# Query pairs taken earlier, keys ahead of the last rotated sum, and a head's ninth block turned later

## The chip, the cores and the metric

The kernel runs on one core of a Trainium2 chip. The metric is the time of one execution on the device in microseconds (us). Before the change it was 1448.48 us, the median of three runs (1446.67 to 1448.85).

Engine names in the rows: PE is TensorE (PEld its weight loads), DVE is VectorE, ACT is ScalarE, POOL is GpSimd, SP is SyncE, which issues most DMAs. Each works through its own queue of instructions in order, and they meet through semaphores.

## The reference

One step of a streaming encoder with two layers over 1024 prompt rows, 16 meta rows and 32 sample rows (1072 columns in all), 8 heads of width 128, in float32.

```
layer 0 (first attention, "fox"):
    h = rmsnorm(x);  q, k, v, f, g = h @ w_in;  logf = log_sigmoid(f + b)
    p = softmax(q k^T / sqrt(128) + cumsum(logf)_q - cumsum(logf)_k, causal)
    x = x + (p v * silu(g)) @ w_out
shared latent, once:
    ckr = rmsnorm(x) @ w_dkv;  c = rmsnorm(ckr[:256]);  kr = rope(ckr[256:320])
layer 1 (second attention, "mla"):
    p = rmsnorm(x) @ w_in
    q = rmsnorm(p[:384]) @ w_uq   ->  per head 128 plain + 64 rotated
    k, v = c @ w_ukv              (128 + 128 a head)
    p = softmax((q_plain k^T + rope(q_rot) kr^T) / sqrt(192), causal by chunks of 64)
    x = x + (p v * silu(gate)) @ w_out
y = rmsnorm(x);  outputs also k, v, logf of layer 0, c and kr
```

The sample rows attend to a cache of 512 rows as well.

## The kernel before

Every float32 operand of a large product is split into a high and a low part, and a product is three matmuls (`three_pass`, L75 to L82: high x high, high x low, low x high). ACT rounds the high part, DVE or POOL subtracts it to get the low part. The order of work on each engine is written out by hand, as loops over the same steps on all engines.

**Attention loops.** For each head h and query tile i (0 to 7, 128 queries; tile i sees i+2 blocks of 128 keys) the loop prepares the scores of the next tile (at i = 7 those of tile 0 of head h+1), turns the probabilities of tile i, and puts products of other kinds between (projections of the next head). In every second step PE also forms the values product of a pair of tiles; the last pair of a head, values(h, 3), comes in step (h+1, 0) behind scores(h+1, 1).

`turn_probs` transposes the probabilities in groups of four blocks (`prob_groups`, L69): 9 blocks at i = 7 make groups of 4, 4 and 1, at i = 4 to 6 there are two groups. Each group goes into one of two PSUM banks in turn, ACT copies it to pT_hi (high part), DVE subtracts and writes pT_lo, and this frees the bank. So group 2 needs the bank of group 0. In the odd steps the groups come before the products of other kinds, in the even steps behind them. `values` waits for the last group.

In the first attention, step i = 7 has two gate chunks of the next head, G(h+1, 0) ahead of the scores and G(h+1, 1) (24 matmuls) behind the turn. In the second attention the three key chunks K(h+1, 0..2) (six matmuls of 348 columns each) all stand in step i = 6, ahead of the turn of tile 6, and `scores` at i = 0 waits for chunks 1 and 2 (in one place, L2059 to L2068). Tiles 0 and 1 read only keys of chunk 0, tile 2 is the first to read chunk 1 (`mla_pieces`, L135). The order of all chunks over the two PSUM banks of projections is `projection_order` (L1460).

**Stage between the attentions** (`latents_pe`, `latents_act`, `latents_dve`, `latents_pool`, `latents_sp`). PE multiplies the input for the query latent (3 blocks), the shared latent (2) and the rotated key (1), then forms four query pairs of heads: per pair n nine chunks of nine matmuls, use 9n + u, in bank (9n + u) mod 8: three "raw" ones (rotated part of both heads) and two times three "nope" ones (plain part of each head). DVE takes each out of its bank, multiplied by q_factor (`take_raw`, `take_nope`, L1776 to L1787); use u waits for the take of use u - 8. The rotation of a pair: SP swaps the halves of `raw` by DMA into `raw_sw`; POOL multiplies by the sine (`turn_sin`), DVE by the cosine (`turn_cos`, into `turned`, one buffer for pairs 1 to 3), DVE adds the two (`turn_add`), ACT rounds (`round_rope`), DVE subtracts (`rope_rest`), and POOL's queue stores both parts (`store_rope`, which waits for `rope_rest`). `take_raw(n)` waits for the swap and the cosine of pair n-1. SP's swap of pair n waits for the sum of pair n-1.

DVE's order between them also holds the norm of the shared latent (`factors`, four instructions to `c_done`), after which ACT rounds it to c_hi and POOL subtracts to c_lo (128x2144). POOL's order at this place: the key's low part, weights of pair 3, store_rope(1), c_lo, weights of the first keys, turn_sin(2), store_rope(2), weights of the first gate, turn_sin(3).

Behind the stage DVE runs `last_rope` (L2426, the sum of pair 3) and then the low parts of key chunks 0 to 2 of head 0. PE's first key chunk waits for c_lo and for all 36 takes, its third for the low part of the first.

Of the kernel before, what the change touches and what calls it, by code (L numbers as in the profile page):

```python
# [27 lines left out]
HEADS = 8  # L28
# [32 lines left out]
S9W = (PAST + SMALL) // 2  # L61

# [146 lines left out]
def fox_heads(nc, m, dram):  # L209
# [23 lines left out]
    with ExitStack() as st:  # L233
# [229 lines left out]
        def _(pe):  # L463
# [145 lines left out]
            def turn_probs(h, i):  # L609
# [4 lines left out]
                for g, blocks in enumerate(prob_groups(i)):  # L614
# [34 lines left out]
            for h in range(HEADS):  # L649
                for i in range(8):  # L650
# [14 lines left out]
                    if i % 2:  # L665
                        turn_probs(h, i)
# [4 lines left out]
                    if i % 2 == 0:  # L671
                        turn_probs(h, i)
# [3 lines left out]
        def _(act):  # L676
# [60 lines left out]
            def turn_probs(h, i):  # L737
                for g, blocks in enumerate(prob_groups(i)):
# [45 lines left out]
            for h in range(HEADS):  # L784
                for i in range(8):
# [6 lines left out]
                    if i % 2:  # L792
                        turn_probs(h, i)
# [10 lines left out]
                    if i % 2 == 0:  # L804
                        turn_probs(h, i)
# [6 lines left out]
        def _(dve):  # L812
# [103 lines left out]
            def turn_probs(h, i):  # L916
                for g, blocks in enumerate(prob_groups(i)):
# [110 lines left out]
            for h in range(HEADS):  # L1028
                for i in range(8):
# [9 lines left out]
                    if i % 2:  # L1039
                        turn_probs(h, i)  # L1040
# [17 lines left out]
                    if i % 2 == 0:  # L1058
                        turn_probs(h, i)
# [412 lines left out]
def latent_attention(nc, m, dram):  # L1472
# [19 lines left out]
    with ExitStack() as st:  # L1492
# [231 lines left out]
        def latents_dve(dve):  # L1724
# [133 lines left out]
        def latents_pool(pool):  # L1858
# [164 lines left out]
        def _(pe):  # L2023
# [35 lines left out]
            def scores(h, i):  # L2059
                n = 8 * h + i  # L2060
                first, pieces, w, used = mla_pieces(i)
                if i == 0:
                    pe.wait_ge(query_split, h + 1)
                    b, nth = proj.bank(("K", h, 1)), proj.nth(("K", h, 1))
                    pe.wait_ge(proj_free[b], nth + 1)
                    b, nth = proj.bank(("K", h, 2)), proj.nth(("K", h, 2))
                    pe.wait_ge(proj_free[b], nth + 1)
                    pe.wait_ge(rope_loaded[h % 2], 32 * (h // 2) + 32)  # L2068
                    if h == 0:
                        pe.wait_ge(k_split, 1)  # L2070
                if n:
# [16 lines left out]
            def turn_probs(h, i):  # L2088
# [4 lines left out]
                for g, blocks in enumerate(prob_groups(i)):  # L2093
# [103 lines left out]
            for h in range(HEADS):  # L2197
                for i in range(8):
                    if h == i == 0:
                        value_block(0, value_blocks(0, 0)[2])  # L2200
                        turn_probs(0, 0)
# [612 lines left out]
```

## Time and profile before

| | |
|---|---|
| median of 3 runs | 1448.48 us |
| the profiled execution | 1449.67 us, its span 1447.9 us |
| TensorE busy | 1322.6 us, 91%, 8651 matmuls |
| VectorE busy | 702.7 us, 49% |
| GpSimd busy | 521.8 us, 36% |
| ScalarE busy | 436.6 us, 30% |
| granted TensorE clock, mean | 0.96 |
| first attention with its start | to about 623 us |
| first output product and stage between | about 626 to 905 us |
| second attention | to about 1308 us |
| second output product and end | to 1447.9 us |

Busy time is the time in which an engine has an instruction at work. Matmuls overlap in the trace: one of 358 columns is listed with 0.33 us but the next one follows after 0.16 us, so the pace is read from the starts. A granted clock of 1.00 is 2.4 GHz, 0.50 is 1.2 GHz. In the timelines the number in brackets is the time for which the engine had nothing to do before the instruction, with what released it.

### The profile page before, as it was taken

What the parts mean: (1) busy time and instruction counts of PE and PEld (TensorE: products, weight loads), DVE (VectorE), ACT (ScalarE), POOL (GpSimd) and SP (SyncE); (2) the same over time, 40 slices, a digit from 0 to 9 for tenths busy, and PEclk for the clock granted to TensorE, in tenths of its full rate; (3) what the DMA queues carried; (4) which work ended last, traced back from release to release, by engine and by line L of the source; (5) the groups of instructions that cost most, each with busy time, mean ns of one, the idle gap of its engine ahead of it and who ended that gap; (6) DMA issues with size and microseconds to landing.
All of it is one profiled execution on the core that took longest, in us unless ns stands there. A gap on an engine that the chain in (4) does not pass through costs nothing. (4 is left out here: it accounts for less than half of the span.)

```text
span 1447.9 us, 21940 instructions
## 1 busy us (share of the span) xinstructions
PE 1322.6 (91%) x8651; PEld 1274.2 (88%) x8651; DVE 702.7 (49%) x1350; ACT 436.6 (30%) x821; POOL 521.8 (36%) x564
## 2 busy tenths in 40 slices
PE   6989999999999999958969996989999999996996
PEld 6989999999999999858969996888989989886996
DVE  5446463446244624634322587356666566663213
ACT  5323232223222322322122322243444344432111
POOL 7434243424352434214663655302222221101541
PEclk9999999999999999989979998989999999997998
DMA  5221212221221120046321157602201222004423
GB/s 197 85 86 52 77 53 81 75 65 57 81 74 61 62 81 31 13 127 211 120 87 62 33 177 228 197 9 65 68 18 54 69 64 59 10 16 140 150 74 134
DMA packets 68398, 123.26 MB, mean 85 GB/s; under 512 B 12576, under 2 KB 43936, under 8 KB 68048
## 3 DMA queue, kind: packets, MB, share of 16 engines
q1 hardware_dynamic: 65872, 113.18, 24.6%
q0 software_dynamic: 2432, 8.78, 2.3%
q8 instruction: 64, 1.05, 0.3%
q14 instruction: 30, 0.25, 0.1%
HBM read 82.24 MB, written 36.95 MB: 82 GB/s over the span
## 5 line engine op out<-in xcount | busy, mean ns | idle before, releaser
L79 PE MATMUL psum<-act,fox_slot_hi 128*128 128x358 f32 (+1 forms) x552 | 184.9, 335 | 11.5 <-DVE act L815 11.4
L80 PE MATMUL psum<-act,fox_slot_hi 128*128 128x358 f32 (+1 forms) x552 | 181.3, 328 | 0.0
L81 PE MATMUL psum<-act,fox_slot_lo 128*128 128x358 f32 (+1 forms) x552 | 180.9, 328 | 0.0
L79 PEld LDWEIGHTS psum<-act,fox_slot_hi 128*128 128x128 f32 x552 | 105.6, 191 | 13.1 <-DVE act L815 13.0
L1101 POOL TENSOR_SCALAR fox_rows<-fox_f_keys,fox_f_query 128x144 f32<-128x144 f32 (+3 forms) x64 | 50.5, 789 | 164.0 <-PE psum L618 163.8
L80 PEld LDWEIGHTS psum<-act,fox_slot_hi 128*128 128x128 f32 x552 | 105.1, 190 | 0.0
L81 PEld LDWEIGHTS psum<-act,fox_slot_lo 128*128 128x128 f32 x552 | 105.0, 190 | 0.0
L720 ACT ACTIVATE fox_rows<-fox_rows,fox_neg_max 128x144 f32<-128x144 f32 (+3 forms) x64 | 50.5, 790 | 103.8 <-DVE fox_neg_max L890 103.0
L79 PE MATMUL psum<-fox_slot_hi,act 128*128 128x256 f32 (+1 forms) x288 | 81.8, 284 | 0.0
L80 PE MATMUL psum<-fox_slot_lo,act 128*128 128x256 f32 (+1 forms) x288 | 81.7, 284 | 0.0
L81 PE MATMUL psum<-fox_slot_hi,act 128*128 128x256 f32 (+1 forms) x288 | 81.6, 283 | 0.0
L742 ACT ACTIVATE fox_pT_hi<-psum 128x512 fp32r<-128x512 f32 (+3 forms) x112 | 52.3, 504 | 93.1 <-PE psum L618 93.1
L1358 PE MATMUL psum<-mix_o_hi,w_hi 128*128 128x358 f32 (+1 forms) x192 | 64.1, 334 | 17.3 <-DVE mix_o_lo L1424 12.8
L1358 PE MATMUL psum<-end_o_hi,end_w_hi 128*128 128x358 f32 (+1 forms) x192 | 63.7, 332 | 15.8 <-DVE end_o_lo L1424 12.8
L922 DVE TENSOR_TENSOR fox_pT_lo<-psum,fox_pT_hi 128x512 fp32r<-128x512 f32 (+3 forms) x112 | 60.7, 572 | 23.2 <-ACT fox_pT_hi L742 21.0
L1087 POOL TENSOR_TENSOR fox_slot_lo<-fox_stage,fox_slot_hi 128x1024 fp32r<-128x1024 f32 x28 | 69.4, 2479 | 2.3
L2265 ACT ACTIVATE mla_pT_hi<-psum 128x512 fp32r<-128x512 f32 (+3 forms) x112 | 52.6, 504 | 56.7 <-PE psum L2098 56.3
L2402 DVE TENSOR_TENSOR mla_pT_lo<-psum,mla_pT_hi 128x512 fp32r<-128x512 f32 (+3 forms) x112 | 60.7, 571 | 11.5 <-ACT mla_pT_hi L2265 9.9
L79 PE MATMUL psum<-act,mla_g_hi 128*128 128x358 f32 (+1 forms) x192 | 65.5, 341 | 0.0
L618 PE MATMUL psum<-ident,fox_rows 128*128 128x128 f32 x352 | 54.3, 281 | 11.2 <-DVE fox_pT_lo L922 9.5
L1359 PE MATMUL psum<-mix_o_lo,w_hi 128*128 128x358 f32 (+1 forms) x192 | 63.7, 332 | 0.0
L1360 PE MATMUL psum<-mix_o_hi,w_lo 128*128 128x358 f32 (+1 forms) x192 | 63.5, 331 | 0.0
(389 smaller groups left out, 4002.5 us busy)
## 6 DMA issues: line engine op xcount, KB each, us to landing
fox_x<-in_xT SPq DMA_DIRECT2D x8, 536.0 KB, 9.7
out<-fox_key SPq DMA_DIRECT2D x8, 536.0 KB, 2.7
mix_o_in<-gated SPq DMA_DIRECT2D x8, 536.0 KB, 4.4
mix_resid<-in_xT SPq DMA_DIRECT2D x8, 536.0 KB, 3.9
resid_b<-mix_resid SPq DMA_DIRECT2D x8, 536.0 KB, 2.7
q_nope<-mla_nope SPq DMA_DIRECT2D x8, 536.0 KB, 6.9
mla_query<-q_nope SPq DMA_DIRECT2D x8, 536.0 KB, 5.9
end_o_in<-gated_b SPq DMA_DIRECT2D x8, 536.0 KB, 4.7
```

Source lines behind the costliest of these rows:

```text
L79: pe.matmul(out, lh, rh, start=start and k == 0, stop=False)
L80: pe.matmul(out, lh, rl, start=False, stop=False)
L81: last = pe.matmul(out, ll, rh, start=False, stop=stop and k == n - 1)
L618: last = pe.transpose(PT[b][:, P * s:P * s + P], rows[n % 3][:, P * k:P * k + P], ident[:, :])
L742: act.activation(pT_hi[:, k:k + n, P * (i % 2):P * (i % 2) + P], PT[b][:, 0:P * n].rearrange("p (a b) -> p a b", b=P), ACT.Copy).then_inc( ...
L922: dve.tensor_tensor(pT_lo[:, k:k + n, cols], PT[b][:, 0:P * n].rearrange("p (a b) -> p a b", b=P), pT_hi[:, k:k + n, cols].bitcast(F32), A ...
L1087: pool.tensor_tensor(lo, src, hi.bitcast(F32), ALU.subtract).then_inc(job_split, 1)
L1358: pe.matmul(out, w_hi[q][:, k, :], o_hi[:, k, col:col + w], start=k == 0, stop=False)
L1359: pe.matmul(out, w_hi[q][:, k, :], o_lo[:, k, col:col + w], start=False, stop=False)
L1360: last = pe.matmul(out, w_lo[q][:, k, :], o_hi[:, k, col:col + w], start=False, stop=k == KT - 1)
L2265: act.activation(pT_hi[:, k:k + n, P * (i % 2):P * (i % 2) + P], PT[b][:, 0:P * n].rearrange("p (a b) -> p a b", b=P), ACT.Copy).then_inc( ...
L2402: dve.tensor_tensor(pT_lo[:, k:k + n, cols], PT[b][:, 0:P * n].rearrange("p (a b) -> p a b", b=P), pT_hi[:, k:k + n, cols].bitcast(F32), A ...
```

## The change

- `turn_probs` takes a slice of the groups on PE, ACT and DVE in both attentions. In steps i = 1, 3, 5 it turns what it did. In step i = 7 it turns groups 0 and 1 at the old place, and group 2 behind the products of other kinds.
- In the second attention key chunk 0 of the next head stays in step 6, chunks 1 and 2 move to step 7, between groups 1 and 2. `scores` of tile 0 waits for chunk 0 alone, that of tile 2 for chunks 1 and 2.
- In the stage between, DVE takes the raw tiles of pairs 2 and 3 ahead of the sum of the pair before, nope(3, 0) ahead of rope_rest(2), and nope(2, 0) and the norm of the latent ahead of rope_rest(1). POOL multiplies the sine of pair 2 ahead of c_lo. DVE takes the low parts of head 0's key chunks ahead of `last_rope`.

```diff
+TURNS_ALL, TURNS_FIRST, TURNS_LAST = slice(0, 3), slice(0, 2), slice(2, 3)
-            def turn_probs(h, i):
+            def turn_probs(h, i, groups):
...
-                for g, blocks in enumerate(prob_groups(i)):
+                for g, blocks in list(enumerate(prob_groups(i)))[groups]:
...
@@ loops of PE, ACT and DVE, first attention (second likewise) @@
                     if i % 2:
-                        turn_probs(h, i)
+                        turn_probs(h, i, TURNS_FIRST)
                     for use in fill[1:] if i == 7 else fill:
                         project(use)
                     if i == 0:
                         small_turn(h)
                     if i % 2 == 0:
-                        turn_probs(h, i)
+                        turn_probs(h, i, TURNS_ALL)
+                    elif i == 7:
+                        turn_probs(h, i, TURNS_LAST)
...
+def keys_due(h, i):
+
+    return {6: [0], 7: [1, 2]}.get(i, []) if h + 1 < HEADS else []
...
@@ projection_order, and the loops of PE, ACT and DVE @@
-            if i == 6 and h + 1 < HEADS:
-                order += [("K", h + 1, c) for c in range(3)]
+            order += [("K", h + 1, c) for c in keys_due(h, i)]
...
@@ latents_dve @@
             take_nope(1, 1)
+            take_raw(2)
             turn_add(1)
             dve.wait_ge(k_done, 1)
             dve.tensor_copy(rope_own[:, :], rope_k[0:ROPE, 0:N_SAMPLE])
-            take_raw(2)
-            rope_rest(1)
             chain(factors(c_factor, 1.0))
...
             last.then_inc(c_done, 1)
             take_nope(2, 0)
+            rope_rest(1)
             turn_cos(2)
             take_nope(2, 1)
+            take_raw(3)
+            turn_add(2)
             dve.wait_ge(c_done, 1)
             dve.tensor_copy(c_own[:, :, :], latent[:, :, 0:N_SAMPLE]).then_inc(own_done, 1)
-            turn_add(2)
-            take_raw(3)
+            take_nope(3, 0)
             rope_rest(2)
-            take_nope(3, 0)
             turn_cos(3)
             take_nope(3, 1)
...
@@ latents_pool @@
             pool.memset(c_lo[:, :, 0:KEY0].bitcast(F32), 0.0)
+            turn_sin(2)
             pool.tensor_tensor(c_lo[:, :, KEY0:KEY0 + T], latent[:, :, :], c_hi[:, :, KEY0:KEY0 + T].bitcast(F32), ALU.subtract).then_inc(c_split, 1)
             rest(KW_STEP, flat(kw_hi), flat(kw_lo), KC * DH)
-            turn_sin(2)
             store_rope(2)
...
@@ scores of the second attention @@
                 if i == 0:
                     pe.wait_ge(query_split, h + 1)
-                    b, nth = proj.bank(("K", h, 1)), proj.nth(("K", h, 1))
-                    pe.wait_ge(proj_free[b], nth + 1)
-                    b, nth = proj.bank(("K", h, 2)), proj.nth(("K", h, 2))
+                    b, nth = proj.bank(("K", h, 0)), proj.nth(("K", h, 0))
                     pe.wait_ge(proj_free[b], nth + 1)
...
+                if i == 2:
+                    for c in (1, 2):
+                        b, nth = proj.bank(("K", h, c)), proj.nth(("K", h, c))
+                        pe.wait_ge(proj_free[b], nth + 1)
...
@@ DVE behind the stage @@
             latents_dve(dve)
-            last_rope()
             for c in range(3):
                 key_chunk(0, c)
+            last_rope()
             last_rope_rest()
```

## Rows read from the trace of the kernel before

**Rows 1.** What TensorE waited for, whole span: us in total, times, longest.

```profile
PE psum L618 <- DVE fox_pT_lo L922: 9.5, 10, 1.5
PE psum L2098 <- DVE mla_pT_lo L2402: 8.3, 9, 1.3
```

**Rows 2.** Timeline of a first-attention seam: start, us, engine, line; last: [idle before].

```profile
149.18 1.72 DVE L922 TENSOR_TENSOR fox_pT_lo<-psum,fox_pT_hi 128x512 fp32r<-128x512 f32 x3 [0.47 <-ACT fox_pT_hi L742]
...
149.92 0.33 PE L618 MATMUL psum<-ident,fox_rows 128*128 128x128 f32 x1 [0.98 <-DVE fox_pT_lo L922]
...
154.04 0.28 PE L79 MATMUL psum<-fox_key_hi,fox_query_hi 128*128 128x272 f32 x1
...
154.24 0.53 DVE L873 TENSOR_TENSOR fox_gate<-psum,rms_cols 128x358 f32<-128x358 f32 x1 [1.80 <-PE psum L81]
...
154.41 0.28 PE L79 MATMUL psum<-fox_pT_hi,fox_value_hi 128*128 128x256 f32 x1
```

**Rows 3.** Timeline of a second-attention seam.

```profile
978.80 0.40 PE L79 MATMUL psum<-mla_c_hi,mla_kw_hi 128*128 128x348 f32 x1 [0.52 <-DVE mla_value_lo L2346]
...
982.16 1.03 PE L2098 MATMUL psum<-ident,mla_probs 128*128 128x128 f32 x8
...
982.85 0.52 DVE L2339 TENSOR_TENSOR mla_key_lo<-psum,mla_key_hi 128x348 fp32r<-128x348 f32 x1 [0.85 <-ACT mla_key_hi L2235]
...
984.26 1.16 PE L2098 MATMUL psum<-ident,mla_probs 128*128 128x128 f32 x8
...
985.56 1.71 DVE L2402 TENSOR_TENSOR mla_pT_lo<-psum,mla_pT_hi 128x512 fp32r<-128x512 f32 x3 [0.62 <-ACT mla_pT_hi L2265]
...
986.30 0.33 PE L2098 MATMUL psum<-ident,mla_probs 128*128 128x128 f32 x1 [0.88 <-DVE mla_pT_lo L2402]
...
987.48 0.36 PE L79 MATMUL psum<-mla_pT_hi,mla_value_hi 128*128 128x256 f32 x1 [0.22 <-DVE mla_pT_lo L2402]
```

**Rows 4.** Timeline of the stage between the attentions, engine by engine.

```profile
865.67 2.52 POOL L1921 TENSOR_TENSOR mla_rope_k_lo<-mla_rope_k,mla_rope_k_hi 128x1072 fp32r<-128x1072 f32 x1
...
865.74 3.58 DVE L1799 TENSOR_TENSOR mla_turned<-mla_turned,mla_raw_sw 128x1072 f32<-128x1072 f32 x1 [2.06 <-POOL mla_raw_sw L1892]
...
869.25 2.65 DVE L1838 COPY mla_rope_own<-mla_rope_k 64x32 f32<-64x32 f32 x1
...
874.31 1.26 DVE L1767 SCALAR_TENSOR_TENSOR mla_c_factor<-mla_square,mla_c_factor 128x1072 f32<-128x1072 f32 x1
...
879.41 1.40 DVE L1774 TENSOR_TENSOR mla_nope<-psum,mla_q_factor 128x358 f32<-128x358 f32 x3
...
879.99 0.43 PE L79 MATMUL psum<-mla_ql,mla_qw_hi 128*128 128x356 f32 x1 [1.49 <-DVE mla_nope L1774]
...
881.95 4.82 POOL L1927 TENSOR_TENSOR mla_c_lo<-mla_latent,mla_c_hi 128x2144 fp32r<-128x2144 f32 x1
...
891.72 0.67 PE L79 MATMUL psum<-mla_ql,mla_qw_hi 128*128 128x356 f32 x1 [2.67 <-DVE mla_raw L1774]
...
897.67 0.40 PE L79 MATMUL psum<-mla_c_hi,mla_kw_hi 128*128 128x348 f32 x1 [2.92 <-DVE mla_nope L1774]
...
902.95 1.27 DVE L2429 TENSOR_TENSOR mla_turned<-mla_turned,mla_raw_sw 128x1072 f32<-128x1072 f32 x1 [5.43 <-POOL mla_raw_sw L1892]
...
904.71 0.66 PE L79 MATMUL psum<-mla_c_hi,mla_kw_hi 128*128 128x348 f32 x1 [3.89 <-DVE mla_key_lo L2339]
...
912.83 0.67 SPq L2017 DMA_DIRECT2D mla_small_rope<-q_rope_small  x1
```

**Rows 5.** Busy us (instructions) of each engine by stretch, granted clock, DMA share, GB/s.

```profile
845.00:877.00 32.00, 32.00 (x198) 32.00 (x197) 29.80 (x31) 10.03 (x9) 16.19 (x9) 1.00 0.57 185
898.00:908.00 10.00, 6.11 (x23) 5.66 (x22) 2.65 (x4) 2.06 (x4) 2.88 (x2) 0.52 1.02 336
620.00:626.00 6.00, 4.43 (x23) 4.07 (x22) 1.58 (x3) 1.08 (x3) 0.00 (x0) 0.72 0.00 0
962.00:1298.00 336.00, 320.43 (x2212) 306.19 (x2210) 208.47 (x482) 138.20 (x306) 65.55 (x104) 1.00 0.18 46
```

More of the change, by code:

```diff
@@ L735, in small_turn, with turn_probs @@
                                ACT.Copy).then_inc(s_turned, 1)
-            def turn_probs(h, i):
-                for g, blocks in enumerate(prob_groups(i)):
+            def turn_probs(h, i, groups):
+                for g, blocks in list(enumerate(prob_groups(i)))[groups]:
                     b, nth = turn.bank((h, i, g)), turn.nth((h, i, g))
@@ L792, in _ @@
                     if i % 2:
-                        turn_probs(h, i)
+                        turn_probs(h, i, TURNS_FIRST)
                     if i < 7:
@@ L804, in _ @@
                     if i % 2 == 0:
-                        turn_probs(h, i)
+                        turn_probs(h, i, TURNS_ALL)
+                    elif i == 7:
+                        turn_probs(h, i, TURNS_LAST)
                     if i == 6 and h + 1 < HEADS:
@@ L914, in small_rescale, with turn_probs @@
                 dve.tensor_scalar(row, row, row_inv_s[:, h % 2:h % 2 + 1], None, ALU.mult).then_inc(s_ready, 1)
-            def turn_probs(h, i):
-                for g, blocks in enumerate(prob_groups(i)):
+            def turn_probs(h, i, groups):
+                for g, blocks in list(enumerate(prob_groups(i)))[groups]:
                     b = turn.bank((h, i, g))
@@ L1039, in _ @@
                     if i % 2:
-                        turn_probs(h, i)
+                        turn_probs(h, i, TURNS_FIRST)
                     if i == 6 and h + 1 < HEADS:
@@ L1058, in _ @@
                     if i % 2 == 0:
-                        turn_probs(h, i)
+                        turn_probs(h, i, TURNS_ALL)
+                    elif i == 7:
+                        turn_probs(h, i, TURNS_LAST)
                     if i == 6 and h + 1 < HEADS:
@@ L2086, in scores, with turn_probs @@
                 last.then_inc(scores_full, 1)
-            def turn_probs(h, i):
+            def turn_probs(h, i, groups):
                 n = 8 * h + i
@@ L2092, in turn_probs @@
                     pe.wait_ge(zeroed, 1)
-                for g, blocks in enumerate(prob_groups(i)):
+                for g, blocks in list(enumerate(prob_groups(i)))[groups]:
                     b, nth = turn.bank((h, i, g)), turn.nth((h, i, g))
@@ L2213, in _ @@
                     if i % 2:
-                        turn_probs(h, i)
+                        turn_probs(h, i, TURNS_FIRST)
                     for c in gate_due(h, i):
                         gate_chunk(h, c)
-                    if i == 6 and h + 1 < HEADS:
-                        for c in range(3):
-                            key_chunk(h + 1, c)
+                    for c in keys_due(h, i):
+                        key_chunk(h + 1, c)
                     if i % 2 == 0:
-                        turn_probs(h, i)
+                        turn_probs(h, i, TURNS_ALL)
+                    elif i == 7:
+                        turn_probs(h, i, TURNS_LAST)
             values(HEADS - 1, 3)
@@ L2258, in exp, with turn_probs @@
                                accum_out=row_sum[:, n % 4:n % 4 + 1]).then_inc(exp_done, 1)
-            def turn_probs(h, i):
-                for g, blocks in enumerate(prob_groups(i)):
+            def turn_probs(h, i, groups):
+                for g, blocks in list(enumerate(prob_groups(i)))[groups]:
                     b, nth = turn.bank((h, i, g)), turn.nth((h, i, g))
@@ L2313, in _ @@
                     if i % 2:
-                        turn_probs(h, i)
+                        turn_probs(h, i, TURNS_FIRST)
                     if i < 7:
@@ L2320, in _ @@
                         value_block(h // 2, t)
-                    if i == 6 and h + 1 < HEADS:
-                        for c in range(3):
-                            key_chunk(h + 1, c)
+                    for c in keys_due(h, i):
+                        key_chunk(h + 1, c)
                     if i % 2 == 0:
-                        turn_probs(h, i)
+                        turn_probs(h, i, TURNS_ALL)
+                    elif i == 7:
+                        turn_probs(h, i, TURNS_LAST)
                     for c in gate_due(h, i):
@@ L2394, in last_turn, with turn_probs @@
                 return (h, i, len(prob_groups(i)) - 1)
-            def turn_probs(h, i):
-                for g, blocks in enumerate(prob_groups(i)):
+            def turn_probs(h, i, groups):
+                for g, blocks in list(enumerate(prob_groups(i)))[groups]:
                     b = turn.bank((h, i, g))
@@ L2458, in _ @@
                     if i % 2:
-                        turn_probs(h, i)
+                        turn_probs(h, i, TURNS_FIRST)
                     if i == 6 and h + 1 < HEADS:
@@ L2475, in _ @@
                         gate_take(h, c)
-                    if i == 6 and h + 1 < HEADS:
-                        for c in range(3):
-                            key_chunk(h + 1, c)
+                    for c in keys_due(h, i):
+                        key_chunk(h + 1, c)
                     if i % 2 == 0:
-                        turn_probs(h, i)
+                        turn_probs(h, i, TURNS_ALL)
+                    elif i == 7:
+                        turn_probs(h, i, TURNS_LAST)
                     for c in gate_due(h, i):
```

2 lines of the change are left out of this document (1 added, 1 removed).

## The prediction

> **What bounds the kernel now.** I read the busy shares first: TensorE is busy for 91% of the span, the others for 49% at most, so only what removes idle time of TensorE (PE below) shortens the run. The list of PE's waits comes next [rows 1]: besides a few long ones at seams of stages, it has two families of short ones, in which the transposes of the first and of the second attention wait for VectorE's (DVE's) low-part copy, up to 1.5 us each, 19 in all. The timeline shows where: at the last tile of a head, nine blocks are turned in groups of 4, 4 and 1 through two PSUM banks, and the third group waits until the first has left its bank: 0.98 us in the first attention [rows 2], 0.88 us in the second [rows 3], at each of 7 head seams. The last list is the timeline of the stage between the attentions (query pairs and shared latent, 833 to 905 us): PE stands still four times, 1.49, 2.67, 2.92 and 3.89 us [rows 4].
>
> **First attention, third group.** The step at i = 7 turned groups 0, 1, 2 and then ran the gate product G1 (24 matmuls). Now G1 stands between groups 1 and 2. The wait of 0.98 us goes: the 3.9 us of G1 hide it. What is late next is values(h, 3), which needs the third group's low part. Call T the moment the last matmul of G1 has been issued; in the trace that is 154.04 [rows 2]. PE needs 0.46 from there: 0.09 for the single transpose (an estimate, eight take 1.03 in all [rows 3]) and 0.37 for scores (154.04 to 154.41). DVE takes G1 first, which is queued ahead of it, from T+0.20 to T+0.73; ScalarE (ACT) is done with the turned block at about T+0.65, and DVE's last piece, 0.3 long, ends at T+1.05. A released PE starts 0.15 later (the first two DVE pieces at 149.18 end near 149.78, the transpose starts at 149.92). So values starts at T+1.20 where it could at T+0.46: a new wait of 0.74. Gain 0.98 - 0.74 = 0.24 a seam, times 7: 1.7 us. Bounds: 0.98 x 7 = 6.9 if the new wait is hidden, -0.3 x 7 = -2.1 if ACT's queue (the small rows' exponential stands ahead) makes it 1.3. I take 1.7, since each piece has its own row. Behind GpSimd's (POOL's) queue stands the bias of tile (h+1, 2), which waits for this group; it comes some 3 us later and still ahead of its reader, for the value product (27 matmuls) runs in between.
>
> **Second attention, third group and keys.** Key chunks 1 and 2 move from step 6 to step 7, behind groups 0 and 1, and the third group follows them. Before, from K0's start to the value product: 987.48 - 978.80 = 8.68 us [rows 3]. After, the pieces of that stretch: K0 1.04 (six matmuls of 0.16, the first 0.08 longer); transposes of tile 6 1.03; then scores(h+1, 0) with its idle time, 1.07 together (983.19 to 984.26) as now, because it waits for K0's low part as it waited for K2's (issue end 982.16, DVE done 982.85 + 0.52 = 1.21 later, 0.2 to PE); from the turn at S = 984.26 groups 0 and 1 take 1.16, K1 and K2 1.92 (12 matmuls of 0.16), the third group 0.09, scores(h+1, 1) 0.87 (986.30 to 987.48 less the 0.22 idle and the transpose). That is 7.18. The new wait: K2's low part ends 1.21 after K2's issue end, the third group's behind it 0.28 later, PE 0.2 later, 1.70 in all, against 0.96 of PE's own work: 0.74. Sum 7.92, gain 0.76; a seam into an even head has no value blocks but the same spacing. Times 7: 5.3, with the restart of matmuls after each stall counted 5.6 us. The bank of group 0 is free 2.04 after S (986.30), and K1, K2 cover to 3.08. Bounds: 0.88 x 7 = 6.2 and a small stall between key chunks on top, 7.2; and nothing, if DVE's order costs 0.8 more at each seam. The scores of tile 2 gain two waits on keys that were finished long before, those of tile 0 lose one: 0 to 0.1 x 7, I take 0. At the end of the last head nothing stands between the groups; nothing changes there.
>
> **The pair stage.** PE issues a chunk (9 matmuls) in 9 x 32/198 = 1.45 us [rows 5] and each chunk needs the bank that DVE took eight chunks earlier. So the order of DVE's queue decides.
> - Raw tiles of pair 2 (chunks 18 to 20) are taken ahead of the sum of pair 1. That sum waited 2.06 for POOL's sine product and then took 3.58 where the like sum at 902.95 takes 1.27 [rows 4]: it ended 1.1 after POOL's k_lo (865.67 + 2.52). The takes read PSUM and fit into this time for nothing; the sum still ends at about 869.3.
> - The 64x32 copy behind it took 2.65 and ended with a POOL subtraction, at 871.9; I leave that. Then rope_rest(1) and the takes are gone from the path, and the two factor and two latent instructions (874.31 to 879.41, 5.10) run 872.05 to 877.15. The nope take follows at once, so chunk 29 is released at 877.7, ahead of its turn at 878.3: the 1.49 go.
> - nope(2,0) 1.40, rope_rest(1) 1.26, turn_cos(2) 1.27, nope(2,1) 1.40, raw(3) 1.40 end at 883.9. Chunk 35 is released at 883.1 and runs from 887.1: the 2.67 go too, and the products end at 888.6.
> - What is late next: POOL was held at store_rope(1) until 879.9 by the moved rope_rest(1), then issues two DMAs (1.1 to 1.3), two memsets (0.4), turn_sin(2) 2.5, to 884.2, and goes straight into c_lo, 4.82 long (881.95), to 889.0. The sum of pair 2 wants the same moment, 884.2, and has two SBUF inputs like that at 865.74: I let it wait to 889.0 and end at 890.15. Then the copy of the own rows behind kw_lo 0.8, nope(3,0) 1.4, rope_rest(2) 1.27, turn_cos(3) 1.27, nope(3,1) 1.4: 896.3. K0 needs the last take; it starts at 896.3, not 897.67: 1.3 gained, with PE idle for 7.7 us in one piece.
> - Key chunks ahead of the last sum: K2 waited 3.89 because DVE sat in last_rope until 904.14 for POOL's sine [rows 4]. ACT has K0's high part by 899.6, so now nothing holds K2. After 7.7 idle I let K0, K1 and K2 run at the low clock (0.29 a matmul, as in the stretch with 0.52 granted [rows 5]): 18 x 0.29 = 5.2, the end at 901.5. Before it was 904.71 + 1.9 = 906.6. The stage hands over 5.1 us earlier, or 6 if G0, whose first 2 us ran at the low clock, is past it: I take 5.5. Bounds: 12.7 (case A) and -1 (the low clock through G0 and G1 too, 48 x 0.13 = 6.2, which eats 5.5 and more). The load of the small rotated query is issued at 912.83 [rows 4]; the sample scores would ask for it near 919, so it stays hidden; its chain starts with last_rope, whose start does not move (902.8).
>
> The lock is the point at which a rule bears on the sum. **The Trainium skill**, "SBUF — State Buffer", section "Who interferes with whom", says that a VectorE instruction with two SBUF inputs and a GpSimd instruction that reads SBUF exclude each other for a whole instruction, whoever issues first. By that rule, the trace agrees: 3.58 us at 865.74 against 1.27, and it speaks against the change, which puts the sum of pair 2 where c_lo starts.
>
> **Sum.** 1.7 + 5.6 + 5.5 = 12.8 us. The profiled execution took 1449.67 (span 1447.9, 1.8 around it) and gives 1436.9; it lies 1.2 over the median of the runs shown, 1448.48, which gives 1435.7.
>
> **Rivals.**
> - A, faster: c_lo does not hold the sum of pair 2 (DVE comes first, or they run together). For: the two want the port in the same 0.1 us. Against: POOL's own next instruction follows without a semaphore. Then the sum ends at 885.4, nope(3,1) at 890.9, K0 follows at 891.0 with the clock high, G0 at 893.9 when its low weights are ready: 12.7 in place of 5.5, 1428.5. 10 in 100.
> - B, the pair stage gives nothing: the stalls only move to the one before K0, and the low clock through G0 and G1 costs 6.2. For: 0.52 granted from 898 to 908 [rows 5]. Against: it recovered within 2 us of steady work there. Only the seams' 7.3 are left: 1441.2. 14 in 100.
> - B', the seams give nothing because the new wait equals the old: 1448.5 - 5.5 = 1443. 3 in 100.
> - C, slower: the clock falls at the head seams. The place: behind values(h, 3)'s new wait. At the end of the first attention, where the waits of the last tile follow each other closely, it fell, 0.72 granted over 6 us, a loss of 0.28 x 6 = 1.7 [rows 5]; at 14 seams 24 us, less 12.8: 1459.5. It decides if a seam's idle is no smaller than there. Against: the seams of now (0.88 and 0.22 within 1.2 us [rows 3]) leave 1.00 over 336 us, and the change lowers the idle. 3 in 100.
> - D, it doesn't do what it says: another engine keeps the third group and K0 at their old times, 1446 to 1450. 4 in 100.
>
> **How the numbers follow.** 66 in 100 for the forecast, 1435.7, whose own range is 1432 to 1439. The range runs from 1428.5 (A) to 1441.5 (B), with the bounds of the three terms mostly inside. A measurement here tells a change of 0.2%, 2.9 us. Faster: 66 + 10 + 14 + 3 = 93; same: 4; slower: 3.
>
> **What would show it.** In the profile after: no wait ahead of the single transposes at 14 seams and a wait of 0.6 to 0.9 ahead of the value product in its place; no wait inside the pair products; one idle of 6 to 9 us ahead of K0; the sum of pair 2 on DVE taking 4 to 6 us; no wait ahead of K2. The prediction is wrong if the value product waits over 1.2 us, if the granted clock at the seams leaves 1.00, or if G0 starts less than 3 us earlier against the first attention's end.

## The result, and the profile after

The changed kernel takes 1425.92 us, the median of 4 runs (1425.23 to 1427.42), against 1448.66 (1446.67 to 1449.51) for the kernel before beside it: ratio 0.9846, interval 0.9829 to 0.9863. The forecast was 1435.7 with a range down to 1428.5, so the direction is right and the size is not: 12.8 us were worked out, 22.3 measured here. Two repeats of the changed kernel, below, give 17.7 and 19.3.

The page's first part, for the profiled execution (busy us, share, instructions):

```profile
span 1424.1 us, 21963 instructions
PE 1314.1 (92%) x8651; PEld 1271.5 (89%) x8651; DVE 700.5 (49%) x1350; ACT 435.9 (31%) x821; POOL 522.3 (37%) x564
```

The matmuls are the same 8651. TensorE's idle time fell from 125.3 to 110.0 us. Its listed busy time fell too, by 8.5 us; 1.7 of that lies between K0 and the third chunk of G0, where fewer matmuls ran at the low clock level. The list of its waits (us in total, times, longest):

```profile
PE psum L80 <- DVE mla_nope L1785: 6.7, 1, 6.7
PE psum L80 <- DVE mla_pT_lo L2417: 6.2, 8, 0.9
...
PE psum L80 <- DVE fox_pT_lo L927: 3.0, 8, 0.7
...
PE psum L619 <- DVE fox_pT_lo L927: 2.7, 3, 1.5
...
PE psum L2111 <- DVE mla_pT_lo L2417: 2.3, 2, 1.3
```

The two families of [rows 1] shrank from 10 to 3 and from 9 to 2 waits. The five that are left all lie in the last head of each attention, where nothing stands between the groups. What grew in their place are the waits ahead of value products (L80): from 1 (0.7 us) to 8 (3.0 us) in the first attention. In the second there were 8 before as well, seven of them short (0.22 in [rows 3]); they grew from 2.5 to 6.2 us. One wait of 6.7 us stands ahead of K0.

Two more rows of the seam of [rows 2] in the kernel before, the eight transposes and the first matmul of G1 (timeline: start, us, engine, line, what, [idle before]):

```profile
147.85 1.09 PE L618 MATMUL psum<-ident,fox_rows 128*128 128x128 f32 x8
...
150.01 0.41 PE L79 MATMUL psum<-act,fox_slot_hi 128*128 128x358 f32 x1
```

The same seam in the changed kernel:

```profile
148.04 1.09 PE L619 MATMUL psum<-ident,fox_rows 128*128 128x128 f32 x8
...
148.89 0.41 PE L80 MATMUL psum<-act,fox_slot_hi 128*128 128x358 f32 x1
...
152.92 0.27 PE L619 MATMUL psum<-ident,fox_rows 128*128 128x128 f32 x1
152.95 0.37 PE L80 MATMUL psum<-fox_key_hi,fox_query_hi 128*128 128x272 f32 x1
...
153.12 0.53 DVE L878 TENSOR_TENSOR fox_gate<-psum,rms_cols 128x358 f32<-128x358 f32 x1 [1.02 <-PE psum L82]
...
153.23 0.28 ACT L745 ACTIVATE fox_pT_hi<-psum 128x128 fp32r<-128x128 f32 x1 [2.28 <-PE psum L619]
...
153.57 0.28 DVE L927 TENSOR_TENSOR fox_pT_lo<-psum,fox_pT_hi 128x128 fp32r<-128x128 f32 x1
...
153.90 0.39 PE L80 MATMUL psum<-fox_pT_hi,fox_value_hi 128*128 128x256 f32 x1 [0.34 <-DVE fox_pT_lo L927]
```

G1 follows the eight transposes without a gap, the single transpose stands behind it and waits for nothing, and the value product waits 0.34. Read the second row against the first: the transposes are listed until 149.13, yet the next product starts at 148.89. The last 0.24 us of this listed stretch is overlap with what follows. The stretch of eight transposes ahead of K1, below, shows the same (967.21 + 1.16 against 968.13).

The seam of the second attention that answers to [rows 3]:

```profile
964.08 0.40 PE L80 MATMUL psum<-mla_c_hi,mla_kw_hi 128*128 128x348 f32 x1 [0.50 <-DVE mla_value_lo L2361]
...
967.21 1.16 PE L2111 MATMUL psum<-ident,mla_probs 128*128 128x128 f32 x8
...
968.13 0.40 PE L80 MATMUL psum<-mla_c_hi,mla_kw_hi 128*128 128x348 f32 x1
...
970.13 0.27 PE L2111 MATMUL psum<-ident,mla_probs 128*128 128x128 f32 x1
...
970.16 0.37 PE L80 MATMUL psum<-mla_key_hi,mla_query_hi 128*128 128x272 f32 x1
...
971.26 0.28 DVE L2417 TENSOR_TENSOR mla_pT_lo<-psum,mla_pT_hi 128x128 fp32r<-128x128 f32 x1
...
971.75 0.36 PE L80 MATMUL psum<-mla_pT_hi,mla_value_hi 128*128 128x256 f32 x1 [0.72 <-DVE mla_pT_lo L2417]
```

From K0's start to the value product it is 7.67 us, where it was 8.68. The waits of 0.88 and 0.22 became one of 0.72.

The stage between the attentions, which answers to [rows 4] (everything ahead of it is 6.1 us earlier in this execution, so 877.40 stands for 883.5 there):

```profile
862.89 2.65 DVE L1850 COPY mla_rope_own<-mla_rope_k 64x32 f32<-64x32 f32 x1
...
877.40 4.81 POOL L1939 TENSOR_TENSOR mla_c_lo<-mla_latent,mla_c_hi 128x2144 fp32r<-128x2144 f32 x1
...
877.49 5.94 DVE L1810 TENSOR_TENSOR mla_turned<-mla_turned,mla_raw_sw 128x1072 f32<-128x1072 f32 x1 [0.41 <-POOL mla_raw_sw L1903]
...
882.16 1.85 POOL L1896 TENSOR_TENSOR mla_kw_lo<-stage,mla_kw_hi 128x256 fp32r<-128x256 f32 x1
...
883.35 0.71 DVE L1863 COPY mla_c_own<-mla_latent 128x64 f32<-128x64 f32 x1
...
887.79 1.39 DVE L1785 TENSOR_TENSOR mla_nope<-psum,mla_q_factor 128x358 f32<-128x358 f32 x3
...
889.33 0.63 PE L80 MATMUL psum<-mla_c_hi,mla_kw_hi 128*128 128x348 f32 x1 [6.72 <-DVE mla_nope L1785]
...
892.66 0.33 PE L80 MATMUL psum<-mla_c_hi,mla_kw_hi 128*128 128x348 f32 x1
...
894.02 0.40 PE L80 MATMUL psum<-act,mla_g_hi 128*128 128x358 f32 x1 [0.23 <-DVE mla_key_lo L2354]
```

The four stalls of the stage became one of 6.72 us, the sum of pair 2 took 5.94 us beside c_lo, and K2 (892.66) waits for nothing. The granted clock around it, and over the second attention (the number behind the instruction counts):

```profile
890.00:891.00 1.00, 1.00 (x5) 1.00 (x5) 0.00 (x0) 0.00 (x0) 1.00 (x2) 0.50 0.88 206
...
892.00:893.00 1.00, 1.00 (x7) 0.97 (x6) 0.51 (x1) 0.14 (x1) 0.92 (x1) 0.84 1.10 412
893.00:894.00 1.00, 0.79 (x5) 0.52 (x5) 0.52 (x1) 0.49 (x2) 0.00 (x0) 1.00 1.10 407
...
945.00:1281.00 336.00, 321.97 (x2242) 310.13 (x2241) 210.97 (x490) 140.27 (x311) 65.62 (x104) 1.00 0.18 47
```

The low level (0.50, 1.2 GHz) ends 3.0 us after K0's start, inside K1; before, the start of G0 (906.62) still ran in it [rows 5]. The seams leave the clock alone: it is 1.00 over the second attention, and 1.00 from 145 to 592 us in the first.

### The profile page after: what moved, and what is told of

The parts are those of the page before. It is cut to its first block and busy times, and to the rows that moved or that the text cites. A ratio compares the mean times of both kernels' runs of the same rounds, so it can differ in the third digit from the quotient of the medians.

```text
span 1424.1 us, 21963 instructions
## 1 busy us (share of the span) xinstructions
PE 1314.1 (92%) x8651; PEld 1271.5 (89%) x8651; DVE 700.5 (49%) x1350; ACT 435.9 (31%) x821; POOL 522.3 (37%) x564
## 3 DMA queue, kind: packets, MB, share of 16 engines
q1 hardware_dynamic: 65872, 113.18, 24.8%
## 5 line engine op out<-in xcount | busy, mean ns | idle before, releaser
L80 PE MATMUL psum<-act,fox_slot_hi 128*128 128x358 f32 (+1 forms) x552 | 185.1, 335 | 11.6 <-DVE act L820 11.6
L80 PEld LDWEIGHTS psum<-act,fox_slot_hi 128*128 128x128 f32 x552 | 105.3, 191 | 13.0 <-DVE act L820 13.0
L80 PE MATMUL psum<-fox_slot_hi,act 128*128 128x256 f32 (+1 forms) x288 | 82.0, 285 | 0.0
L80 PE MATMUL psum<-act,mla_g_hi 128*128 128x358 f32 (+1 forms) x192 | 65.0, 339 | 0.2 <-DVE mla_key_lo L2354 0.2
L81 PE MATMUL psum<-act,mla_g_hi 128*128 128x358 f32 (+1 forms) x192 | 63.2, 329 | 0.0
```

The source lines that it names most:

```text
L80: pe.matmul(out, lh, rh, start=start and k == 0, stop=False)
L81: pe.matmul(out, lh, rl, start=False, stop=False)
```

## The experiments

Twelve experiments ran. Times are medians with the lowest and highest of the runs. The ratio is to the kernel before, run beside it on the same chip, with its 95% interval. The experiments ran on three chips, on which the kernel before took 1446.07, 1448.34 and 1447.43, so lines of the table are compared by ratio, or directly where the kernel before beside them is the same.

| kernel | us (range, runs) | before beside it | ratio |
|---|---|---|---|
| changed, second time | 1428.22 (1426.27 to 1430.24, 4) | 1446.07 | 0.9878 [0.9860, 0.9895] |
| changed, third time | 1427.91 (1425.05 to 1433.30, 6) | 1447.43 | 0.9867 [0.9843, 0.9891] |
| first-attention seams alone | 1441.17 (1438.24 to 1442.48, 6) | 1446.07 | 0.9962 [0.9946, 0.9978] |
| second-attention seams alone | 1440.62 (1435.76 to 1442.27, 6) | 1446.07 | 0.9959 [0.9943, 0.9975] |
| both seams, no pair stage | 1433.78 (1430.67 to 1438.22, 6) | 1447.43 | 0.9906 [0.9884, 0.9927] |
| pair stage alone | 1442.18 (1439.48 to 1446.24, 12) | 1446.07 | 0.9973 [0.9962, 0.9984] |
| only the first keys ahead | 1441.31 (1438.26 to 1446.19, 6) | 1448.34 | 0.9954 [0.9936, 0.9971] |
| changed, sum of pair 2 ahead of c_lo | 1428.75 (1424.59 to 1432.00, 5) | 1448.34 | 0.9871 [0.9851, 0.9890] |
| changed, G1's take last | 1427.86 (one) | 1447.43 | none |
| changed, third group between, second attention | 1421.83 (1418.03 to 1424.85, 5) | 1447.43 | 0.9821 [0.9800, 0.9843] |
| the same in both attentions | 1419.34 (1417.36 to 1420.30, 5) | 1448.34 | 0.9802 [0.9786, 0.9819] |

The twelfth is one more execution of the kernel before.

**The changed kernel, unaltered,** twice.

> The changed kernel once more, unaltered, to see which parts of its gain come back in a second profile. Theory (work moved, stalls gone): 1426 us; the seams of both attentions gain 4.1 and 7.0 us and the pair stage 6.5 to 7.4 against the kernel before, each within 0.3. Theory for the other 5 us (first output product 2.0, sample rows and first tiles of the second attention 1.2, from the last value product to the end 2.1): if they follow from where the low clock falls, they come back too, within 0.5 each; if they were chance of one profile, they change by 1 to 2 us here.

> The changed kernel unaltered, a third time, with fresh runs of the kernel before on the same chip. Theory (the mechanisms give 18 us, what the first comparison showed beyond that is scatter between executions): ratio 0.987 to 0.9885, as in the second comparison. Rival (the change is worth 22 us and the second comparison was the odd one): ratio under 0.986.

Measured: 0.9878 and 0.9867, which are 17.7 and 19.3 us of 1448.5, against 22.3 in the first comparison. The third ratio lies between the theory's 0.987 and the rival's 0.986 and decides for neither. All three intervals touch each other near 0.986. The first comparison is at the favourable end. Of what the first pair of traces showed beyond the changed places, the 1.4 us in the first output projection did not come back in the second trace (195.5 us against 195.0 in the kernel before), and of the 2.1 behind the last value product half did.

**The kernel before, once more.**

> The kernel before once more, with a profile, to see how far untouched stages differ between two profiles of one kernel. Theory (the gain outside the changed places was chance of two profiles): the first output product, the sample rows and the end differ from the first profile by 1 to 2 us, the seams and the pair stage by less than 0.3. Rival (the change shortens these stages too): all stages within 0.5.

It took 1446.08 us with a span of 1444.3, 3.6 less than in the trace that the forecast was worked out from. Neither the theory nor the rival came true as written. The first output projection differs by 0.2 us and the end by 0.4, where 1 to 2 were expected; the pair stage ahead of K0, where under 0.3 was expected, is 1.5 shorter (61.90 against 63.41). Single executions differ by as much as one of the forecast's terms, so a difference of two traces as wholes sizes nothing here. What can be sized is a stretch that repeats, over all traces with and without an edit. I took the start of the same TensorE instruction in every trace: value product 3 of head 0 to that of head 6 (six seams) in each attention, the first pair product to K0, and K0 to G0's third chunk. The two rows of seams repeat within 0.6 us but for one trace; the two rows of the pair stage scatter by 1.1 to 1.5 without the edit.

| stretch, us | without the edit | with it |
|---|---|---|
| six seams, first attention | 435.55 to 435.70 in five, mean 435.60 | 432.09 to 432.37 in eight, mean 432.18 |
| six seams, second attention | 275.28 to 276.40 in five, mean 275.56 | 269.23 to 269.81 in seven, mean 269.48 |
| first pair product to K0 | 61.90 to 63.41 in five, mean 62.7 | 60.97 to 61.36 in seven, mean 61.1 |
| K0 to G0's third chunk | 20.89 to 22.00 in five, mean 21.5 | 16.34 to 16.69 in seven, mean 16.6 |

That is 0.57 a seam in the first attention, 1.01 in the second, and 1.6 + 5.0 in the pair stage. With seven seams each: 4.0 + 7.1 + 6.6 = 17.7 us. The stage with the first output projection, which no kernel here alters, takes from its first product to the first pair product 195.0 in the first trace of before, 193.6 in the first of after, and 192.9 to 198.1 in the others: much of the scatter is there.

**One part at a time.** Four kernels: only the third group of the first attention moved, only the loops of the second attention, only the pair stage, and both attentions without the pair stage. In short:

```
first:   turn_probs(h, i, TURNS_FIRST) ... project(use) ... turn_probs(h, i, TURNS_LAST)
second:  keys_due(h, i) = {6: [0], 7: [1, 2]}, and the same split of turn_probs
pair:    take_raw(2), turn_add, rope_rest, turn_sin(2) and last_rope() as in the change
```

> Only the third turn group of the first attention is moved behind G1; second attention and pair stage are as before. Main theory: 7 seams of 0.6, 4.1 us, ratio 0.9972; if the first output product's 2 us hang on this shift, 6 us, 0.9958. Rival (my prediction's arithmetic, 0.24 a seam): 1.7 us, 0.9988.

> Only the second attention's loop is changed (key chunks 1 and 2 and the third group moved to step 7). Main theory: 7 seams of 1.0, 7.0 us, plus up to 2 at the end of the kernel, 7 to 9 us, ratio 0.9938 to 0.9952. Rival (0.76 to 0.8 a seam as predicted): 5.3 to 5.6 us, 0.9962.

> Only the stage between the attentions is changed (order of takes and sums on DVE, sine of pair 2 on POOL, key chunks ahead of last_rope). Main theory: 7 to 8.6 us (6.5 to 7.4 to the first gate chunk, 1.2 in the sample rows), ratio 0.9941 to 0.9951, since the low clock ends before the third key chunk. Rival (predicted 5.5): 0.9962. Rival, no lock between DVE and POOL: over 12 us; the first trace after speaks against it, since the sum of pair 2 took 5.94.

> The changed kernel with the pair stage and the first keys as in the kernel before: both families of head seams are moved, nothing else. Theory (the three parts add up, each as its own run showed): 7 x 0.59 in the first attention and 7 x 1.00 in the second, 11.1 us, so 1435 to 1439 beside 1447 for the kernel before (ratio 0.992 to 0.994), about 7 above the changed kernel. Rival (the parts hide each other, and the surplus over the forecast is an interaction): a saving of under 8 us here, or within 3 us of the changed kernel.

The ratios are worth 5.5, 5.9, 3.9 and 13.6 us, each uncertain by 1.6 to 3.2. In the traces the first gives -3.4 over its six seams and nothing at the others', the second -6.2 and nothing in the first attention, the pair stage the lengths of the table. The stretches of one part do not move with the others, so the parts are independent there, and the two seam edits together (13.6, interval 10.6 to 16.8) hold the 11.1 of their stretches. As whole runs the experiments say less. The first rules out the forecast's 1.7 us (ratio 0.9988). The second can't tell 7 us from the rival's 5.3 to 5.6. The two seam edits gave more than was expected (0.9906, expected 0.992 to 0.994), the pair stage less (0.9973, expected 0.9941 to 0.9951). With the pair stage alone the run as a whole gained 3.9 us (interval 2.3 to 5.5), where the stretch gained 7.6 against the first trace of before and 6.7 against the mean. In its trace the second attention, which it doesn't alter, is 1.0 longer than in the kernel before, in two of its six heads, and the end behind it 1.2 against the first trace of before; why is open. Two other comparisons hold the stage and give more: the changed kernel lies 5.9 us below the one with the seams alone beside it (1427.91 and 1433.78), and the next experiment gives 6.7 for one line of the stage.

**Only the first keys ahead of the last rotated sum,** and all else as before:

```
-            last_rope()
             for c in range(3):
                 key_chunk(0, c)
+            last_rope()
             last_rope_rest()
```

> Only the key chunks of head 0 are put ahead of last_rope on VectorE; all other orders are those of before. Theory: the first key chunk starts where it did, the wait of 3.89 us ahead of the third goes, and the low clock ends earlier: the first gate chunk starts 4 to 5 us earlier, ratio 0.9965 to 0.9975. Rival (the wait moves to the sample scores, whose loads hang on the last rotated sum): 0 to 2 us.

Its timeline at K0, K2 and G0:

```profile
899.83 0.63 PE L79 MATMUL psum<-mla_c_hi,mla_kw_hi 128*128 128x348 f32 x1 [3.72 <-DVE mla_nope L1774]
...
903.45 0.49 PE L79 MATMUL psum<-mla_c_hi,mla_kw_hi 128*128 128x348 f32 x1
...
905.15 0.33 PE L79 MATMUL psum<-act,mla_g_hi 128*128 128x358 f32 x1
```

K2 has no wait. From K0 to G0's third chunk it is 16.9 us, which is 4.6 of the 5.0 that the whole pair stage gains there. The first gate chunk comes 3.1 us earlier against the mean of the five traces without the edit, where 4 to 5 was expected; the rest comes within that chunk. The whole run gained 6.7 us (interval 4.2 to 9.3), more than expected, but the interval holds the 4.6. One moved call does most of the stage's work, and the reordering of the pair's takes adds 1.6 ahead of K0 and little behind it.

**The lock.** In the changed kernel GpSimd waits for the sum of pair 2 before it starts c_lo (arguments shortened):

```
+            pool.wait_ge(rope_ready, 3)
             pool.tensor_tensor(c_lo, latent, c_hi, ALU.subtract)
```

> The changed kernel, but GpSimd waits for the sum of pair 2 before it starts the low part of the latent (c_lo). If the two exclude each other for whole instructions: the sum takes 1.27 us instead of 5.94, the copy of the own rows behind it (0.71 now) takes the wait, 4 to 5 us, or GpSimd's instruction does, the first key chunk starts within 0.5 us of where it did, and the time stays within 1 us of the changed kernel's. Rival (the sum is slow for another reason): it stays at 5 to 6 us, and the key chunk is 1 to 2 us later. Rival (only the sum is held, the copy is not): the key chunk starts 4 us earlier.

Its timeline:

```profile
877.86 1.28 DVE L1810 TENSOR_TENSOR mla_turned<-mla_turned,mla_raw_sw 128x1072 f32<-128x1072 f32 x1 [0.39 <-POOL mla_raw_sw L1903]
...
879.05 0.19 DVE L1863 COPY mla_c_own<-mla_latent 128x64 f32<-128x64 f32 x1
...
879.22 4.83 POOL L1940 TENSOR_TENSOR mla_c_lo<-mla_latent,mla_c_hi 128x2144 fp32r<-128x2144 f32 x1 [1.39 <-DVE mla_turned L1810]
...
881.41 1.10 ACT L1680 ACTIVATE mla_rope_hi<-mla_turned 128x1072 fp32r<-128x1072 f32 x1 [8.03 <-DMA q_rope_lo<-mla_rope_lo]
...
882.55 2.62 DVE L1814 TENSOR_TENSOR mla_rope_lo<-mla_turned,mla_rope_hi 128x1072 fp32r<-128x1072 f32 x1 [2.00 <-ACT mla_rope_hi L1680]
```

The same sum takes 1.28 us alone and 5.94 beside c_lo: the lock is shown. But K0 comes only 1.3 us earlier (59.85 after the first pair product, against 61.1; expected within 0.5), and the run is no faster, 1428.75. The wait was expected to pass to the copy behind the sum or to c_lo, and it passed to neither; two other things held K0. ScalarE rounds the sum into the buffer that GpSimd's queue still stores for pair 1, and starts when that store has landed (881.41), 2.3 us after the sum. And the next VectorE instruction with two SBUF inputs, the low part of the rotated rows, waits 2.00 for ScalarE and then falls into c_lo itself (2.62 in place of 1.26). Rival A, 12.7 us for this stage, would have needed both out of the way as well.

**What the new wait of the first attention hangs on.** The forecast counted VectorE's take of G1, which is queued ahead of the last piece. This kernel puts the take behind it.

> The changed kernel with VectorE's take of the gate product G1 moved behind the third group's low part in the first attention. The forecast put the new wait ahead of values(h, 3) down to that take, which stands ahead in VectorE's queue. Theory (the trace after says ScalarE's copy, done about 0.05 before the take ends, is as late): the listed wait of 0.34 shrinks by at most 0.1. Rival (the take is what makes it late): the wait goes to under 0.15.

```profile
152.20 0.27 PE L619 MATMUL psum<-ident,fox_rows 128*128 128x128 f32 x1
...
152.51 0.28 ACT L745 ACTIVATE fox_pT_hi<-psum 128x128 fp32r<-128x128 f32 x1 [2.28 <-PE psum L619]
...
152.81 0.29 DVE L927 TENSOR_TENSOR fox_pT_lo<-psum,fox_pT_hi 128x128 fp32r<-128x128 f32 x1 [1.44 <-ACT fox_pT_hi L745]
...
153.16 0.39 PE L80 MATMUL psum<-fox_pT_hi,fox_value_hi 128*128 128x256 f32 x1 [0.32 <-DVE fox_pT_lo L927]
```

The wait goes from 0.34 to 0.32. VectorE now stands idle until ScalarE's copy is done. What remains is the chain transpose, ScalarE, VectorE, TensorE, 0.96 us from start to start (152.20 to 153.16), and the order on VectorE changes nothing in it. The next two kernels put the transpose earlier.

**The third group between products,** not behind them all: between K1 and K2 in the second attention, and in the next kernel also behind 5 of the 8 terms of G1 in the first.

```
             for c in keys_due(h, i):
+                if c == 2:
+                    turn_probs(h, i, TURNS_LAST)
                 key_chunk(h + 1, c)
```

```
+                if between is not None:
+                    three_pass(pe, PJ[b][:, 0:w], terms[:5], stop=False)
+                    between()
+                    three_pass(pe, PJ[b][:, 0:w], terms[5:], start=False).then_inc(proj_full[b], 1)
...
+                    if i == 7 and fill:
+                        columns(*fill[1], between=lambda: turn_probs(h, i, TURNS_LAST))
```

On VectorE the second of them also puts the third group's piece ahead of the take of G1.

> The changed kernel with the third group of the second attention between key chunks K1 and K2 in place of behind both; the first attention as in the changed kernel. Theory (the new wait ahead of the value product, listed as 0.72 to 0.91, is what is left of the seam): 0.73 us a seam less, 5.1 in all, ratio to before about 0.984. Rival (DVE's low part of K1 is queued behind the third group's and holds the scores): under 2 us less than the changed kernel.

> The changed kernel with the third turn group inside G1 (behind five of its eight terms) in the first attention and between key chunks 1 and 2 in the second, VectorE and ScalarE in the same order. Theory (the new wait ahead of the value product is the third group's way through ScalarE and VectorE behind the last product): the waits go, 0.5 to 0.6 a seam, 14 seams, 7 to 8 us below the changed kernel, ratio to before 0.982 to 0.984. Rival (the waits are set by the queue of VectorE, which has as much to do as before): under 2 us, 0.987.

The single transpose, VectorE's piece and the value product of a seam in the second attention, with both moved:

```profile
967.87 0.30 PE L2117 MATMUL psum<-ident,mla_probs 128*128 128x128 f32 x1
...
969.07 0.28 DVE L2427 TENSOR_TENSOR mla_pT_lo<-psum,mla_pT_hi 128x128 fp32r<-128x128 f32 x1
...
969.59 0.36 PE L80 MATMUL psum<-mla_pT_hi,mla_value_hi 128*128 128x256 f32 x1
```

and its waits ahead of value products, all heads:

```profile
PE psum L80 <- DVE mla_pT_lo L2427: 0.9, 1, 0.9
...
PE psum L80 <- DVE fox_pT_lo L933: 0.7, 1, 0.7
```

Seven waits of each family are gone. The six seams of the second attention take 10.5 us less than in the kernel before (1.76 each), those of the first 7.1 (1.19 each). Against the changed kernel that is 0.74 and 0.62 a seam, 9.5 us over 14 seams. The kernel with the second attention alone lies 6.1 us below the changed one beside it (expected 5.1; 0.73 a seam in its trace). The one with both is the fastest of all, 1419.34 us; its ratio, 0.9802, is better than the theory's 0.982 to 0.984, which counted 0.5 to 0.6 a seam. Both rivals, under 2 us, fall. Against each other the intervals of the two kernels overlap; what the first attention adds is read from its stretch.

## Why the forecast was right, and where it failed

**First-attention seams, forecast 1.7, measured 4.0.** This term failed most: the mechanism came as written, but the step "Gain 0.98 - 0.74 = 0.24 a seam" has both of its sizes wrong. The 0.98 was the listed wait. The list counts from the listed end of the transposes, and 0.24 of that is overlap. Between starts, the stall before was 149.92 - (147.85 + 0.85) = 1.22, where 0.85 is what eight transposes take until the next product in the kernel after (148.04 to 148.89). The 0.74 was charged with a restart of 0.15, where TensorE starts 0.05 after VectorE's listed end (153.85 to 153.90), and with pieces that each end a little later than the next one can start: with T, the end of G1's issue, at 152.92, the forecast's T + 1.20 was T + 0.98. Between starts the new wait is 0.95 - 0.37 = 0.58. With 0.06 for the transpose (it delays the next product by 0.03 in place of 0.09) the seam gives 1.22 + 0.06 - 0.58 = 0.70, and it does so in all seven seams: 5.86 us from the eight transposes to the value product, where it was 6.56. A part of it is lost right behind: after the wait the value product's second matmul starts 0.22 after its first, where it was 0.12. So 0.57 a seam is left over the stretch. The bound above, 0.98 a seam, held; the forecast took the piece-by-piece sum, whose errors all had one sign.

**Second-attention seams, forecast 5.6, measured 7.1.** The path from K0's start was forecast at 7.92 and is 7.67. Its pieces: 3.13 to the groups (forecast 3.14), groups 0.92 (1.16), K1 and K2 2.00 (1.92), transpose 0.03 (0.09), scores and new wait 1.59 (1.61). The error is the 0.24 at the end of the listed stretch of transposes; the others cancel. The new wait was right: 0.72 listed, 0.74 forecast. The 0.3 us that the forecast added for restarts had no row, and this seam shows none beyond the pieces.

**Pair stage, forecast 5.5, measured 6.6.** Every step came as written: no waits inside the products, the copy at 2.65, the sum of pair 2 blocked by c_lo (5.94; the forecast let it end at 890.15, and in the old trace's times it ended at 889.5), one idle ahead of K0 (6.72, forecast 7.7), no wait ahead of K2. K0 came 0.9 earlier than 896.3 in the first trace. The clock term was off: I charged all 18 key matmuls at the low level, 5.2, and 10 to 13 of them ran in it in the seven traces with this order; with the gap of 0.23 ahead of G0, K0 to G0 took 4.69. G0 then ran at full clock, and up to its third chunk that is 1.1 more than K0 to G0 alone gained. On the mean of the traces both halves are a little better than worked out, 1.6 for 1.3 and 5.0 for 4.2. **The Trainium skill**, "SBUF — State Buffer", section "Who interferes with whom", says that a VectorE instruction with two SBUF inputs and a GpSimd instruction that reads SBUF exclude each other. By that rule, both traces agree: 5.94 beside c_lo and 1.28 with c_lo held back.

**The sum.** 17.7 us from the stretches against 12.8: of the 4.9 that were missing, 2.3 lie in the first attention, 1.5 in the second and 1.1 in the pair stage. With them the forecast would have been 1430.8, inside the range. The two later comparisons, 17.7 and 19.3, agree with it. The first comparison's 22.3 lies 4.6 above. Its interval, 19.8 to 24.8, does not reach 17.7, and no run finds a mechanism for the surplus. The two first traces are 23.8 us apart. What they have beyond 17.7 lies in pieces: 1.0 in the pair stage, 0.7 behind the last seam of the first attention, 1.4 in its output projection, 1.0 between G0 and the second attention's first seam, 2.1 after the last value product, nearly all of it where both kernels have the same instructions. That is consistent with scatter; it is not shown to be only that. So the time fell below the range for two reasons: the mis-sized stalls, which the runs show, and the surplus of the first comparison, whose cause stays open.

**The rivals.** A fell: the lock held, and with it lifted for the sum K0 came 1.3 us earlier, not A's 5.3, since a store and the next locked instruction took over the wait. B fell: the pair stage gave 6.6 and the low level ended before G0. The prediction's argument against B, that the clock recovered within 2 us of steady work, misread the trace before: steady work began with K2 at 904.71, and the clock was low over 904 to 908 and 0.64 over 908 to 909, so it took about 4. (B's time is 1441.2, as in its own line, not the range's 1441.5.) B' fell with 0.57 and 1.01 a seam. C fell: 1.00 granted over both attentions' seams. D fell.

## What to carry to other kernels

Size a stall from start to start: from where the next instruction of the engine would have started, which a seam without a stall shows, to where it did. The listed idle leaves out the overlap at the end of a run of short matmuls, and over 14 seams 0.24 us is 3.4 us. When a transposed block must pass two engines before it is used, put its transpose the length of that chain (0.96 us here) ahead of the reader and fill both sides; reordering VectorE's queue within the chain gave 0.02. Before lifting a lock, look for the next thing that the freed instruction's followers wait for: here 4.7 us at one sum were worth 1.3 at K0. And move the one call that holds a queue before reordering the queue around it: 4.6 of the pair stage's 6.6 us came from one line.

## What the runs showed of the hardware

- Eight transposes are listed at 1.09 to 1.16 us, and the next product starts 0.85 to 0.92 after their start. A single one is listed at 0.27 to 0.33 and delays the next product by 0.03 to 0.06 between products, by 0.09 behind a wait (149.92 to 150.01).
- TensorE starts 0.05 us after the listed end of the VectorE instruction that it waits for at the value products of the first attention, 0.15 at K0 and 0.21 at the value product of the second (971.54 to 971.75). A value product that waited starts its second matmul 0.22 after the first, one that did not 0.12.
- A VectorE instruction of 1.28 us took 5.94 beside a GpSimd instruction of 4.81 that started 0.09 earlier. A copy of 128x64 behind it took 0.71 and ended with GpSimd's next instruction (884.06 and 884.01); with GpSimd held back it took 0.19.
- After an idle of 6.3 to 6.7 us TensorE ran 3.0 to 3.9 us at the low level (matmuls every 0.29), in seven traces. After 5.1 (c_lo held back) it ran 5.1 us, and after 3.7 (only the keys moved) 5.3; in the last the level had already fallen before that idle, 0.71 granted from 894 to 896. A longer idle was not followed by a longer slow stretch.
- The kernel before took 1443.1 to 1452.6 us over all its runs here, and the stage with the first output projection, which no kernel alters, 192.9 to 198.1.
